# Swapping the V row and the U row in each pair of gathers of a PEER layer

## The reference, cut to what matters

```python
def block(args):                     # 128 tokens at a time, kk = 8 heads * 16
    xb, ib, gb = args
    act = jax.nn.gelu(jnp.einsum('tkd,td->tk', expert_u[ib], xb))
    return jnp.einsum('tk,tkd->td', act * gb, expert_v[ib])
```

## Time and profile before

| | |
|---|---|
| median of 3 runs | 2485.25 us (2483.07 to 2485.45) |
| the profiled execution, its own time | 2483.89 us |
| its span | 2482.5 us |
| first gather asked for, last one landed | 332.34 us, about 1685.6 us |
| DMA rate from 680 to 1630 us | 421 GB/s, DMA engines busy 1.01 of the time |
| TensorE, VectorE, ScalarE, POOL busy over the span | 85%, 57%, 26%, 27% |

### The profile page before, as it was taken

How to read it: one execution, slowest core, us unless ns; L and a number is a source line. 1 busy time by engine, 2 the same in 40 slices (tenths; PEclk the granted TensorE clock), 3 DMA queues, 4 the chain that set the end, 5 groups by cost and what they waited for, 6 DMA issues and landing times.

```text
span 2482.5 us, 19393 instructions
## 1 busy us (share of the span) xinstructions
PE 2106.7 (85%) x7532; PEld 1345.7 (54%) x7532; DVE 1411.8 (57%) x1786; ACT 644.2 (26%) x884; POOL 682.2 (27%) x522
## 2 busy tenths in 40 slices
PE   8998948698887787777777777779999999999999
PEld 7876845254432332222222222226888778888887
DVE  4576686645568777454444444445554665654454
ACT  5454522111112010100000000004443353543342
POOL 0000045445455555444454545430000000000000
PEclk9999978999999999999999999989999999999999
DMA  7443469899999999999999999994455544455553
GB/s 274 157 153 104 168 272 398 358 421 397 372 422 421 421 421 422 421 422 421 421 422 422 421 422 422 422 404 160 183 189 194 177 161 170 170 191 195 191 179 143
DMA packets 105355, 751.22 MB, mean 303 GB/s; under 512 B 11952, under 2 KB 11952, under 8 KB 14384
## 3 DMA queue, kind: packets, MB, share of 16 engines
q0 software_dynamic: 73728, 536.90, 52.3%
q1 hardware_dynamic: 29376, 207.63, 23.4%
q10 hardware_dynamic: 2160, 5.45, 0.6%
HBM read 747.84 MB, written 2.10 MB: 302 GB/s over the span
## 4 chain that ended last, share of the span: by engine, by line
PE 51%; DMA 35%; DVE 9%; issue 2%; ACT 1%; POOL 1%; ACTq 0%; SPq 0%; DVEq 0%; POOLq 0%
PE ps L336 37%; DMA xT_rows<-in_expert_v,idx 23%; PE ps L647 10%; DMA wlo_row<-in_expert_v,idx 4%; DMA W<-in_expert_u,idx 2%; DMA xT_rows<-in_expert_u,idx 2%; DMA W<-in_expert_v,idx 2%; DVE wlo L1254 1%; DMA raw<-in_expert_u,idx 1%; DVE raw L1635 1%; PE ps L357 1%; DVE W L1635 1%; PE ps L545 1%; DVE xT_rows L1635 1%; ACT whi L818 1%
## 5 line engine op out<-in xcount | busy, mean ns | idle before, releaser
L336 PE MATMUL ps<-whi,xT 128*128 128x512 f32 x2736 | 664.8, 396 | 14.3 <-ACT whi L818 11.5
L1254 DVE TENSOR_TENSOR wlo<-raw,whi 128x2048 fp32r<-128x2048 f32 x195 | 445.4, 2288 | 282.5 <-ACT whi L818 282.3
L336 PEld LDWEIGHTS ps<-whi,xT 128*128 128x128 f32 x2736 | 515.4, 190 | 130.2 <-issue 15.0
L818 ACT ACTIVATE whi<-raw 128x2048 fp32r<-128x2048 f32 x195 | 372.2, 1914 | 474.4 <-PE ps L336 371.5
L647 PE MATMUL ps<-xT_rows,W 128*128 128x512 f32 x808 | 379.1, 612 | 126.4 <-DMA xT_rows<-in_expert_v,idx 121.5
L336 PE MATMUL ps<-wlo,xT 128*128 128x512 f32 x1368 | 341.0, 392 | 32.5 <-DVE wlo L1254 32.5
L647 PEld LDWEIGHTS ps<-xT_rows,W 128*128 128x128 f32 x808 | 147.8, 193 | 355.0 <-issue 263.8
L1635 DVE CUSTOM_DVE_ANT_0 xT_rows<-xT_rows,W 128x2048 f32<-128x2048 f32 x96 | 219.9, 2291 | 206.2 <-DMA xT_rows<-in_expert_u,idx 205.8
L647 PE MATMUL ps<-W 128*128 128x512 f32 x536 | 255.9, 621 | 90.6 <-DMA W<-in_expert_v,idx 66.2
L336 PEld LDWEIGHTS ps<-wlo,xT 128*128 128x128 f32 x1368 | 257.7, 189 | 88.0 <-DVE wlo L1254 34.5
L647 PE MATMUL ps<-raw,W 128*128 128x512 f32 x512 | 236.1, 604 | 61.7 <-DMA raw<-in_expert_v,idx 56.8
(11 more groups left out here) (275 smaller groups left out, 1469.6 us busy)
## 6 DMA issues: line engine op xcount, KB each, us to landing
raw<-in_weights SPq DMA_DIRECT2D x196, 1024.0 KB, 4.9
h<-in_x SPq DMA_DIRECT2D x8, 256.0 KB, 6.3
out<-h ACTq DMA_DIRECT2D x8, 256.0 KB, 2.8
xT_rows<-in_expert_v,idx POOLq DMA_INDIRECT x106, 15.8
xT_rows<-in_expert_u,idx POOLq DMA_INDIRECT x96, 16.4
W<-in_expert_u,idx POOLq DMA_INDIRECT x70, 16.4
raw<-in_expert_u,idx POOLq DMA_INDIRECT x70, 16.4
W<-in_expert_v,idx POOLq DMA_INDIRECT x70, 15.5
```

What stands on the lines that cost most here:

```text
L336: return pe.matmul(ps[:, (banks_of(b) if bank is None else bank) + t, 0:cols_n], x[:, q0 + qn * 4 + k, s], w_[:, cs], start=start, stop=stop)
L818: a.activation(split_into(c)[0], raw[:, RAW_OF[c], :], ACT.Copy).then_inc(sem["hi_done"], 1)
L1254: v.tensor_tensor(lo, raw[:, RAW_OF[c], :], hi.bitcast(F32), ALU.subtract).then_inc(sem["lo_done"], 1)
```

## The change

In each pair the V row is asked for first and then the U row of the next unit. The first 16 and the last 16 places stay as they are. `FEW_ROWS` is computed from the place of u(4,0), which becomes 113, so v(3,0) at place 112 goes to the last of the six slots; V rows take the even places and U rows the odd ones, and the slots of the two kinds are exchanged. Nothing else is edited.

```diff
 ROW_ORDER = ([("u", unit, j) for unit in range(LAG) for j in range(16)]
-             + [(kind, unit, j) for p in range(UNITS) for j in range(16) for kind, unit in (("u", p + LAG), ("v", p)) if unit < UNITS])
+             + [(kind, unit, j) for p in range(UNITS) for j in range(16) for kind, unit in (("v", p), ("u", p + LAG)) if unit < UNITS])
```

## The result

The changed kernel takes 2495.43 us (median of 6 runs, 2492.77 to 2497.64) against 2485.35 for the kernel before (6 runs, 2483.07 to 2486.74): a ratio of 1.0040, 95% interval 1.0028 to 1.0053. It is 10.1 us slower, where I forecast -0.4 us and a range up to 2489.5. The profiled execution has a span of 2491.4 us, 8.9 more than before; it was the fastest of its six runs.

The account below looks back on a forecast made before the run. The gathers were taken as bounded by DMA bytes at 421 GB/s, so only idle DMA time counted. Terms 0 + 0 + 0.2 + 0 + 0.4 - 1.0 = -0.4 us gave 2484.9 us against 2485.25, range 2480.8 to 2489.5.

Parts of the forecast that it names:

- Parts 1 and 2: Steady pairs, and unit heads in the long stretch: the swap costs 0 at each, as queued requests cover the shifts.
- 4 to 6 us given as a sign: At each unit's head, the wait of TensorE for ScalarE's diagonal that the profile after should show.
- cover of 10.3 us: Steady pairs: queueing, by which a request may come later before the DMA engines run dry; 15.8 us landing against 5.5 idle.
- Part 3: Start of the pairs: U rows stand behind V requests, some 3 to 4 us later; +0.2 us, bounds 0 and +0.7.
- Part 2: Unit heads, long stretch: v(p,0) waits about 5.0 us more in its slot, covered by queueing; 0.
- Part 4: Two waits for chosen experts: a later U row and a V row fetched meanwhile cancel; 0 each, bounds -0.5 and +0.5.
- Part 5: Right after the first wait: v(1,3) ahead of u(2,3) leaves a gap of 0 to 2.5 us; taken as +0.4.
- Eight slots cover it: After the second wait: eight slots are free instead of six, which covers the delay seen behind the first wait.
- Part 6: The tail: v(15,1) and the 14 after it asked for 3 us earlier; -1.0 us, ends -2.4 and +1.
- (a): Both waits for experts: each hides a whole fetched row, -5.0 us, about 2477.8 us in all; chance 0.07.
- (b): Heads of units 0 to 2, six slots: not covered, up to 5.0 us each, 2492.4 us; chance 0.08.
- its own condition of 10.5: Six-slot unit heads: the loss occurs where a V row lands less than 10.5 us after its request (5.5 + 5.0).

Follow-up runs that it names:

- weights-first kernel: The changed kernel with each unit's weights made ahead of the dot of the next unit's first U row, at every unit: 2490.91 us, ratio 1.0019.
- its control: The kernel before with the same edit, a unit's weights made ahead of the dot of the next unit's first row: 2485.60 us, ratio 0.9996.

## Why the prediction was wrong, by its steps

**Parts 1 and 2** (steady pairs, unit heads in the long stretch: 0) were right. TensorE's wait for the diagonal grew by the 5.0 us worked out (6.76 against 1.78, so above the 4 to 6 us given as a sign), and the cover of 10.3 us held: waits of 10.34 us in POOL, a lower clock for a row, and still 419 GB/s; with units 4 to 15 swapped alone, +0.3 us.

**Part 3** (+0.2, bound +0.7) failed most. It measured +2.6 in the profile and +3.6 with unit 0's pairs alone, so its bound was wrong too. I saw that U rows go "behind the V request they stood ahead of, some 3 to 4 us later", and then priced it as a share of the time that was lost there before (0.97 of 138 us). A share already lost says nothing of what a later request adds: the engines were busy 1.02 of the time from 400 to 410 us with that U row in the queue, and 0.76 without it. The question to ask was Part 2's, how long is the queue when POOL stops, and here it was short: v(0,0) had landed 9.5 us after its request, 4.0 over an idle landing, and rows 24 to 33 of the kernel before 6.6 to 10.6 us after theirs, while POOL stood 4 to 5 us at TensorE's slot. The kernel with one more U row ahead confirms the sign from the other side: 1.0 us earlier at row 47, -5.1 us by the medians.

**Part 4** (0 at each wait) was right at the first: u(1,15) later, v(1,0) fetched in exchange, row 52 at +1.9 where rows 34 to 47 stood at +2.6. The two halves were seen apart, +2.7 without the fetched row (unit 0 alone, row 47 to row 52) and -2.7 without the later U row (units 1 to 3 alone). At the second it failed: +2.5, and the bound was +0.5. Counted from the first gather u(4,0) went out 9.3 us later; 4.2 of these were there before, and the other 5.1 are a row's time, which v(3,0) gives back, and 2.6 of POOL's pause ahead of request 113, which the trace of before held in plain view, between u(4,0) and v(3,0), and which the swap put between the choice and u(4,0). I had taken u(4,0)'s delay after the index write from a row that had no pause in it. The delay of the request is shown; that it is worth all of the 2.5 us isn't, as kernels without the swap there lose 0.4 to 2.0 us in the same rows.

**Part 5** (+0.4, bound 2.5) was right in its mechanism and mis-sized: +2.5. The request came as worked out: v(1,3) 14.9 us after u(2,0), where I had 14.4 (493.9 less 479.5). The step that failed is the last one, the 0.4 taken out of a gap of 0 to 2.5 us because a weight chunk would fill part of it: SP issued its next loads only at 496.03, 0.4 us ahead of the landing of row 53, the last one asked for ahead of v(1,3) (492.80 in the kernel before, 2.9 us ahead of it), the engines were busy 0.62 of the time from 495 to 500 us, and the U row behind v(1,3), asked for 16.6 us after u(2,0) instead of 8.9, came in late as well. It is the gap's whole bound. (The sum "or 495" had left out the chunk that it names.) The weights-first kernel took the step away, and its control shows that it is the swap's own. "Eight slots cover it" behind the second wait was wrong by 1.0 us (+6.7 at row 119, +7.7 at row 135), if that is no drift.

**Part 6** (-1.0) gave 0. The stretch from the landing of row 487 to VectorE's start on the last row took 69.7 us in both kernels. Busy times in it, kernel before, then the changed one:

```profile
1615.80:1685.50 69.70, 52.75 (x100) 19.40 (x100) 29.82 (x26) 5.88 (x17) 19.85 (x19) 0.90 0.96 395
```

```profile
1623.40:1693.10 69.70, 47.31 (x96) 17.46 (x94) 32.10 (x29) 5.87 (x17) 18.33 (x18) 0.93 0.98 409
```

The idle time did shrink, but 409 against 395 GB/s over 69.7 us is 1.0 MB more, in size one of SP's weight chunks, as the rows in both stretches are the same number: the time gained went into a load, it seems, and not into rows. Which transfers took the rows' turn was not tried. The forecast delay was there: u(15,15) was used 8.7 us after the U row before it instead of 4.9, with SP's four loads in the queue, and v(15,1) was asked for at 1649.71, only 1.6 us earlier than before once the kernel's own 7.6 us of lateness are taken off, where I had 3. By the rule of the Trainium skill, "DMA: Bandwidth & Descriptors", section "Queues, rings and completion order", that queues with work are served in turn, I had worked out 0 for the tail, and 0 it was; that it came about for that reason isn't shown.

**The rivals.** (a) was half right: a fetched row is a gift, if the U row that the choice waits for stays where it is, which this change doesn't do. (b) named the right six-slot stretch and the right wait, 7.5 us in all; 4.5 us of the loss are of its kind by the medians of the weights-first kernel, 2.5 by its trace. I gave it 0.08 and set against it that "from 480 to 570 the engines were full": again a share of before in place of a length of queue. The first wait had emptied the queue: u(2,0) and v(1,0) landed 5.5 and 7.5 us after their requests in the kernel before, under its own condition of 10.5. About 1.1 us between rows 135 and 487 and 1.4 us behind the gathers stay open; both are within the drift between two profiled executions. That the two kinds exchange slots and that the six slots last one row longer came with the swap and was not tried apart.

**The range.** Its upper end added 0.7, 2.5 and 1 but left out Part 4's own +0.5 and the 1.2 us of scatter by which the lower end was widened. With both it is 2491.2, still below the 2495.43 measured.

## What to carry to other kernels

When one queue asks for rows of two kinds and must wait for one consumer's slots, put the row that doesn't depend on that consumer ahead of the wait, and price a reordering by how many rows are in flight while the issuer stands still, not by how busy the engines were. A wait for data can be filled with transfers whose operands are known already, but only as many as slots can hold without delaying what follows the wait, and with the row that ends the wait left in its place. Here one U row more ahead at the start made -5 us and one less +5 (+10 with the other units); V rows in the waits made -6 us (one), -14 (two, with the U row more at the start), -2 (four) and +31 (four, kept through the unit). The busy shares of the kernel before foretold none of these.

## What was not expected of the hardware

POOL pauses at a few of its gathers for nothing that the profile shows: ahead of request 113 in all 14 kernels here, and later 106 requests apart, ahead of 221, 327 and 433 where u(4,0) is request 112, of 332 and 438 where it is 113, and of 333 and 439 where it is later; full-length ones take 3.66 to 3.69 us of idle time. So the first place is the same for every order and the later ones aren't. In three kernels the later idle times are shorter (0.94 to 1.55 us). What makes the pause is open; one more instruction ahead of the loop didn't shift it. A rival for the cause that nobody tried is the loading of instructions: a packet of the instruction queue (q14) starts 3.5 us ahead of request 113 in the changed kernel and 3.9 us ahead in the kernel before, but none within 8 us ahead of their later pauses.

After an idle wait the DMA engines need more than one row to be back at their pace: in the kernel before u(2,0) landed 5.5 us after its request and the next row 3.3 us behind it, the ones after 2.5 us apart.

Behind a wait of 6 to 15 us TensorE takes longer for the next row: in the changed kernel 14 such rows ahead of the tail took 5.1 to 6.8 us instead of 3.67. The granted clock was 0.57 of full speed over the row at 1092.78 us, so it ran mostly at the lower level (1.2 GHz), and 1.00 (2.4 GHz) from 1065 to 1085 us. Where slots are few, that is part of the price of a V row that comes too early.
